# Own-engine waits only at data dependencies, new rests by layer, an early product with p_2, and layer 2 opened in quarters

## The chip, the core and the metric

The kernel runs on one core of a Trainium2 chip. The metric is the time of one execution on the device, in microseconds (us). TensorE is called PE, VectorE DVE, ScalarE ACT, GpSimd POOL and SyncE SP. "Clock" is TensorE's granted clock: 1.0 is 2.4 GHz, 0.5 is 1.2 GHz.

## What is computed

Two stacked networks over 256 tokens of width 2048, batch 1, all in float32. The first block has two layers; each is a modulation by a condition vector, an input projection of 6144 columns, a state-space mixer (S5) beside a differential attention, and an output projection. The second block has one layer: an RWKV-7 mixer beside a latent attention (MLA), an output projection, a convolutional feed-forward, and a product with a per-layer embedding `p_2`. Cut to the lines that matter here:

```python
for l in range(DEPTH):                                   # DEPTH = 2
    mod = c_act @ w_ada[l] + b_ada[l]
    shift, scale, gate = jnp.split(mod, 3, axis=-1)
    h = rms_norm(x, norm_g[l]) * (1.0 + scale[:, None, :]) + shift[:, None, :]
    proj = h @ w_in[l]
    u, z_s, q, k, v, z_a = jnp.split(proj, splits, axis=-1)
    y_s = s5_mixer(u, ...) * jax.nn.silu(z_s)
    y_a = diff_attention(q, k, v, ...) * jax.nn.silu(z_a)
    x = x + gate[:, None, :] * (jnp.concatenate([y_s, y_a], axis=-1) @ w_out[l])
x = rms_norm(x, final_g)
# second block
u = rms_norm_2(h, pre_mix_norm[i])
z = u @ w_in[i]
y_rw, y_mla = rwkv7_mixer(z_rw, ...), mla_mixer(z_mla, ...)
mix = (g_rw * (y_rw @ w_branch_rw[i]) + g_mla * (y_mla @ w_branch_mla[i])) @ w_out[i]
h = h + rms_norm_2(mix, post_mix_norm[i])
u = rms_norm_2(h, pre_ffn_norm[i])
up = causal_dwconv(u @ w_up[i], conv_w[i], conv_b[i])
gate, val = jnp.split(up, 2, axis=-1)
f = (gelu(gate) * val) @ w_down[i]
h = h + rms_norm_2(f, post_ffn_norm[i])
e = p[i] @ w_ple[i]
h = h + rms_norm_2(sigmoid(h @ w_ple_gate[i]) * e, ple_norm[i])
```

## The kernel before

**Products.** Activations lie transposed: 16 row blocks of 128 features by 256 tokens. Every large matrix is streamed as halves of 128x1024 numbers, eight 128x128 blocks each. ACT writes the high part of a half (`hi`, line 944) and DVE the rest (`lo`, line 941), and PE makes three products per block, high by high, high by rest, rest by high (`mm`, lines 988 and following). "A block" below is these three products of 128x256. Four halves can be split ahead of the one in use (`NS = 4`); the high part is made three halves ahead, the rest one beat later (`split_ahead`, `rest`).

**The order is written out beforehand.** `Timeline.run` makes one list of beats, and each engine's program walks through that list and emits its own part of each beat. All five queues are in order, so a beat's place in the list decides what stands in front of what on each engine. `stream(...)` lays a projection block by block. After every `per` blocks it calls `bg()` once, and each background generator (S5, its tail, attention, the next layer's modulation, RWKV, MLA) advances by one round. A generator adds a beat and then yields as many rounds as its "rest" says: with `per=2` one round of rest puts two blocks of product between two steps of a chain. `drain(...)` runs rounds with no product between them until the generator has ended.

**Rests.** They are tuples in `s5_prepare` (9 steps), `s5_follow` (8), `attention` (15) and `rwkv` (15 steps, for each of 8 pairs of heads), the same for both layers. PE's part of attention stands at steps 0, 7, 9 and 13, that of `s5_follow` at 0, 2, 4 and 6, that of `rwkv` at 0, 3 to 14. `s5_phases` places a DVE step and, some rounds later, three sines on ACT. After `rwkv` come `rw_seq` and `rw_post` (group norm: means, squares, variances, a root, scaling), and `drain(gr)` stands behind the stream they lie in.

**Order of the blocks.** An ordinary projection takes all 16 row blocks k of one tile of 128 columns, then the next tile. `PAIRS` names streams whose first two tiles are taken in halves: tile 0 with k 0 to 7, tile 1 with k 0 to 7, then k 8 to 15 of both. `QUADS` names streams whose first four tiles are taken in quarters: k 0 to 3 of four tiles, then k 4 to 7, and so on. Layer 2's input projection (`("w_in", 48)`) is in `PAIRS`.

**Waits on the own engine.** On ACT and DVE, every instruction but the splits calls `Port.begin()` (line 924), which waits until the newest earlier instruction of that engine has told of its end. `wait_ge` adds the waits on others. The splits (`apart_high`, `apart_low`) have none on their own engine.

**Between w_out2 and w_up.** After `w_out2` come the norm's sums (`rms`), `recip`, then for four groups of rows `scale`, `post` (the sum into x), four `hf` (the split of the new rows) and `sqf` (squares). The product with `p_2` (`w_ple`, 32 blocks) lies between `w_up`'s second half and `w_down1`; its operand is split at `w_up`'s end.

Of the kernel before, what the change touches and what calls it, by code (L numbers as in the profile page):

```python
# [173 lines left out]
MO = BK  # L174
_c = Cursor(BASE)
FO, FT, EM, PP = (_c.alloc(n) for n in (4096, 1536, 4096, 512))
FH = NF

# [63 lines left out]


# [42 lines left out]
PAIRS = (("w_in", 48), ("w_in2", 0), ("w_up", 0))  # L286

QUADS = (("w_pg", 0),)
# [11 lines left out]
class Timeline:  # L300
# [160 lines left out]
    def stream(self, name, l, u0, n0, nt, nk, per=8, late=None):  # L461
# [3 lines left out]
        for blk in range(nt * nk):  # L465
# [9 lines left out]
            if blk % 8 == 0:  # L475
                if (name, n, k) == ("w_up", 87, 8):
                    self.spared = p
                    for i in range(2):
                        self.add("part", "p", i)
# [16 lines left out]
            if k == nk - 1:  # L496
                held.append(t)
            if late is not None and blk == (71 if quads else 39):
# [42 lines left out]
    def s5(self, l):  # L541
# [8 lines left out]
        for x in self.s5_prepare(l, 0):  # L550
            yield
        for x in self.s5_phases(l, 0):
# [3 lines left out]
        for _ in range(6):  # L556
# [36 lines left out]
    def s5_phases(self, l, p):  # L593
        for _ in range(10 if p else 0):
            yield
        self.add("s5_phase", l, p)
        for _ in range(4):
# [14 lines left out]
    def s5_prepare(self, l, b):  # L612
        for i, rest in enumerate((1, 2, 2, 5, 3, 4, 1, 2, 0)):
# [4 lines left out]
    def s5_follow(self, l, b):  # L618
        for i, rest in enumerate((2, 3, 1, 5, 2, 3, 1, 2)):
# [35 lines left out]
    def rwkv(self):  # L655
# [74 lines left out]
    def run(self):  # L730
# [35 lines left out]
        for l in range(2):  # L766
# [15 lines left out]
            self.mod_rest = 2  # L782
# [3 lines left out]
            self.mod_rest = 5  # L786
# [10 lines left out]
            self.mod_rest = 2  # L797
# [93 lines left out]
class Op:  # L891


    def __init__(self, port, ins, chained=True):
        self.port, self.ins, self.told, self.chained = port, ins, False, chained

    def then_inc(self, sem, *keys):
# [3 lines left out]
        if self.chained:  # L901
            p.newest, self.told = (sem, p.n[sem]), True
# [4 lines left out]
class Port:  # L907


    def __init__(self, signals, name, e, m, in_order):  # L910
# [1911 lines left out]
```

## Time and profile before

| | |
|---|---|
| median of 3 runs | 3105.74 us (3104.97 to 3106.44) |
| the profiled execution | 3101.39 us |
| its span, first to last instruction | 3099.6 us |
| PE busy | 2911.4 us, 94% of the span |
| DVE busy | 2148.8 us, 69% |
| ACT busy | 1535.5 us, 50% |
| mean granted clock | 0.976 |

PE is the busiest engine by far, but "busy" contains stretches at half clock. The parts of the page and the views on which the prediction rests stand below, in its order.

### The profile page before, as it was taken

The numbers are of one execution on the slowest core, as the hardware profiler recorded it, in microseconds if no ns is written. First come the engines' busy times: TensorE is split into PE (matmuls) and PEld (weight loads), VectorE is DVE, ScalarE is ACT, GpSimd is POOL, SyncE is SP. The second block draws the span as 40 slices with busy tenths as digits, with TensorE's granted clock in tenths as the row PEclk, the third lists the DMA queues.
The fourth block names the chain that finished last, engine by engine and source line by source line (L and its number), as shares of the span: only waits on it lengthen the run. The fifth ranks groups of instructions, "written<-read, shape, count | busy, mean of one in ns | idle before, by whom it ended". The sixth has DMA issues, their size and how long they took to land.

```text
span 3099.6 us, 59134 instructions
## 1 busy us (share of the span) xinstructions
PE 2911.4 (94%) x24112; PEld 2695.1 (87%) x24112; DVE 2148.8 (69%) x3498; ACT 1535.5 (50%) x2404; POOL 284.4 (9%) x488
## 2 busy tenths in 40 slices
PE   6899999998999999999999999999899999999987
PEld 2578777788988889999888888999899999999987
DVE  6367777687788877766665667675888746887465
ACT  3335555365555655644343434545555544555454
POOL 0012212100122220200000010010000000000000
PEclk9899999998999999999999999999999999999999
DMA  9887776884645455554333334555455555555543
GB/s 376 309 264 256 248 266 232 286 287 158 179 153 164 155 182 194 177 181 157 107 108 110 115 117 137 163 178 184 134 190 185 186 184 180 181 187 177 184 151 116
DMA packets 168223, 580.91 MB, mean 187 GB/s; under 512 B 40272, under 2 KB 40304, under 8 KB 155536
## 3 DMA queue, kind: packets, MB, share of 16 engines
q1 hardware_dynamic: 146784, 525.40, 51.1%
q0 software_dynamic: 20592, 48.26, 5.1%
q8 instruction: 190, 3.11, 0.4%
q10 hardware_dynamic: 576, 3.47, 0.3%
q14 instruction: 81, 0.66, 0.1%
HBM read 555.22 MB, written 21.76 MB: 186 GB/s over the span
## 4 chain that ended last, share of the span: by engine, by line
PE 68%; DVE 15%; DMA 7%; ACT 5%; issue 4%; SPq 1%; POOL 0%; DVEq 0%; ACTq 0%
PE acc L988 67%; DVE arena L948 6%; ACT arena L985 3%; DVE upper L948 2%; DVE arena L958 1%; DMA arena<-in_w_ada 1%; DMA arena<-scr_k 1%; DVE rounded L941 1%; DMA arena<-in_w_in 1%; DMA scr_k<-arena 1%; DVE upper L958 1%; PE acc L991 1%; DMA upper<-in_w_ada 1%; ACT L985 1%; ACT upper L985 1%
## 5 line engine op out<-in xcount | busy, mean ns | idle before, releaser
L988 PE MATMUL acc<-rounded 128*128 128x256 f32 x14688 | 1913.1, 289 | 33.4 <-issue 14.3
L988 PEld LDWEIGHTS acc<-rounded 128*128 128x128 f32 x14688 | 1820.8, 194 | 117.1 <-issue 88.0
L944 ACT ACTIVATE rounded<-arena 128x1024 fp32r<-128x1024 f32 x802 | 847.7, 1059 | 735.4 <-PE acc L988 554.5
L941 DVE TENSOR_TENSOR rounded<-arena,rounded 128x1024 fp32r<-128x1024 f32 x802 | 974.8, 1225 | 247.0 <-ACT rounded L944 246.7
L988 PEld LDWEIGHTS acc<-upper_rounded,rounded 128*128 128x128 f32 x4560 | 551.8, 193 | 16.2 <-issue 14.0
L988 PE MATMUL acc<-upper_rounded,rounded 128*128 128x256 f32 x4560 | 557.7, 284 | 1.4 <-DVE rounded L941 0.9
L985 ACT ACTIVATE arena<-arena 128x256 f32<-128x256 f32 (+4 forms) x477 | 251.3, 527 | 226.3 <-DVE arena L948 143.1
L948 DVE TENSOR_TENSOR arena<-arena 128x256 f32<-128x256 f32 (+5 forms) x458 | 244.0, 533 | 46.2 <-ACT arena L985 33.2
L948 DVE TENSOR_TENSOR arena<-acc,arena 128x256 f32<-128x256 f32 (+4 forms) x270 | 117.2, 434 | 222.7 <-PE acc L988 213.2
L988 PE MATMUL acc<-arena 128*32 128x512 f32 (+8 forms) x1550 | 214.5, 487 | 51.4 <-DVE arena L948 23.0
L958 DVE SCALAR_TENSOR_TENSOR arena<-arena 128x256 f32<-128x256 f32 (+6 forms) x465 | 208.1, 448 | 51.0 <-ACT arena L985 35.3
L985 ACT ACTIVATE arena<-acc 128x256 f32<-128x256 f32 (+3 forms) x275 | 103.0, 374 | 199.1 <-PE acc L988 186.7
L988 PE MATMUL acc<-upper 128*128 128x128 f32 (+7 forms) x1568 | 184.9, 300 | 12.9 <-DVE upper L948 8.3
L988 PEld LDWEIGHTS acc<-arena 128*32 128x32 f32 (+3 forms) x1550 | 85.5, 140 | 114.5 <-DMA arena<-in_w_ada 46.2
L988 PEld LDWEIGHTS acc<-upper 128*128 128x128 f32 (+4 forms) x1568 | 144.5, 168 | 33.4 <-DVE upper L948 10.1
L985 ACT ACTIVATE upper<-acc 128x256 f32<-128x256 f32 (+4 forms) x176 | 88.0, 500 | 142.8 <-PE acc L988 100.8
L985 ACT ACTIVATE arena<-acc,arena 128x256 f32<-128x256 f32 (+1 forms) x148 | 63.3, 428 | 81.0 <-PE acc L988 76.0
L988 PE MATMUL acc<-upper,arena 64*64 64x64 f32 (+4 forms) x482 | 62.4, 352 | 28.2 <-DMA upper<-in_w_ada 8.2
L938 POOL DMA_DIRECT2D arena<-scr_k x128 | 77.3, 620 | 106.7 <-DMA scr_k<-arena 106.2
L991 PE MATMUL acc<-arena 128*128 128x128 f32 x384 | 71.0, 279 | 16.7 <-ACT arena L985 13.1
L948 DVE TENSOR_TENSOR upper<-upper,acc 128x512 f32<-128x512 f32 (+2 forms) x48 | 33.1, 689 | 76.8 <-PE acc L988 76.0
L938 POOL DMA_DIRECT2D scr_g<-arena x56 | 30.4, 545 | 517.8 <-DVE arena L962 270.1
(94 smaller groups left out, 1260.2 us busy)
## 6 DMA issues: line engine op xcount, KB each, us to landing
arena<-in_w_in SPq DMA_DIRECT2D x328, 512.0 KB, 4.6
arena<-in_w_ada SPq DMA_DIRECT2D x88, 1024.0 KB, 5.4
arena<-in_w_up SPq DMA_DIRECT2D x176, 512.0 KB, 4.1
arena<-in_w_down SPq DMA_DIRECT2D x88, 512.0 KB, 3.9
arena<-in_w_outa SPq DMA_DIRECT2D x32, 512.0 KB, 6.7
arena<-in_w_glu SPq DMA_DIRECT2D x32, 512.0 KB, 6.2
arena<-in_w_outm SPq DMA_DIRECT2D x32, 512.0 KB, 4.6
arena<-in_w_out SPq DMA_DIRECT2D x32, 512.0 KB, 4.3
```

The source lines that it names most:

```text
L938: self.e.dma_start(out, in_).then_inc(self.signals.sems[sem], 16)
L941: return Op(self, self.e and self.e.tensor_tensor(o, a, b, SUB), False)
L944: return Op(self, self.e and self.e.activation(o, a, ACT.Copy), False)
L948: return self.put(self.e and self.e.tensor_tensor(o, a, b, op))
L958: return self.put(self.e and self.e.scalar_tensor_tensor(out=o, in0=a, scalar=s, in1=b, op0=o1, op1=o2))
L985: return self.put(self.e and self.e.activation(o, a, f, scale=scale, **kw))
L988: return self.put(self.e and self.e.matmul(o, l, r, start=start, stop=stop, skip_group_check=True))
L991: return self.put(self.e and self.e.transpose(o, i, self.m.con("ident")))
```

## The change

- `Port.begin()` goes. DVE and ACT wait for their own engine only where a `settle()` is written out (64 places on DVE, and one at the end of ACT's program) or where a keyed wait names the instruction whose data is used (for example `("parts", l, b)`, `("aa", i)`, `("scaled", tag, g)`).
- The rests become tables, by layer for S5 and attention. `s5_phases` of layer 2 starts only when tile 0 of layer 2's input projection is evacuated. The modulation's rest (`mod_rest`) is 2 throughout; it was 2, 5, 2.
- Layer 2's input projection goes from `PAIRS` to `QUADS`, and its weights are packed accordingly.
- `w_ple` moves up between `w_out2` and `w_up`. Its beats surround those of the norm and of the first three groups of rows; the last group and all four squares come after eight blocks of `w_up`. The load and the split of `p_2` move ahead of that. Buffers move: `MO` to `AR`, the squares to `SQF`, `p_2`'s parts to `PT`.

```diff
-PAIRS = (("w_in", 48), ("w_in2", 0), ("w_up", 0))
-
-QUADS = (("w_pg", 0),)
+PAIRS = (("w_in2", 0), ("w_up", 0))
+
+QUADS = (("w_in", 48), ("w_pg", 0))
+
+S5_PREP = ((0, 1, 3, 6, 1, 6, 1, 2, 0),
+    (1, 2, 2, 4, 3, 3, 3, 1, 0))
+S5_RUN = ((1, 3, 1, 6, 2, 3, 2, 1),
+    (1, 4, 3, 6, 2, 1, 1, 1))
+S5_PHASE = ((13, 5),
+    (17, 2))
+S5_START = (6, 8)
+ATTENTION = ((1, 2, 4, 2, 3, 2, 4, 1, 3, 1, 1, 2, 2, 2, 1),
+    (1, 1, 2, 1, 2, 2, 4, 1, 5, 2, 2, 3, 3, 2, 1))
+RWKV = (1, 3, 3, 6, 3, 4, 2, 2, 2, 1, 2, 2, 2, 4, 1)
+MOD_REST = (2, 2, 2)
...
+        while l and ("w_in", 1, 0) not in self.marks:
+            yield
         for x in self.s5_phases(l, 0):
...
-        for i, rest in enumerate((1, 2, 2, 5, 3, 4, 1, 2, 0)):
+        for i, rest in enumerate(S5_PREP[l]):
...
-        for i, rest in enumerate((2, 3, 1, 5, 2, 3, 1, 2)):
+        for i, rest in enumerate(S5_RUN[l]):
...
-            for i, rest in enumerate((2, 2, 2, 2, 2, 2, 4, 2, 2, 2, 1, 2, 2, 2, 1)):
+            for i, rest in enumerate(ATTENTION[l]):
...
-            for s, rest in enumerate((1, 2, 3, 5, 3, 3, 2, 2, 2, 2, 2, 2, 2, 2, 1)):
+            for s, rest in enumerate(RWKV):
...
-        self.stream("w_out2", 0, 0, 0, 16, 16)
-        self.rms("mo", ("w_out2", 0, 15))
-        self.ready("w_up", 0)
-        self.add("recip", "mo")
-        for g in range(4):
-            self.scaled("mo", g)
+        self.add("ff_first")
+
+        def parts():
+            for i in range(2):
+                self.add("part", "p", i)
+
+        self.stream("w_out2", 0, 0, 0, 16, 16, between={63: parts})
+
+        def root():
+            self.add("recip", "mo")
+            self.scaled("mo", 0)
+
+        def rows(g):
             for k in range(4 * g, 4 * g + 4):
                 self.add("hf", k)
-            self.add("sqf", g)
-        self.add("ff_first")
+            if g < 3:
+                self.scaled("mo", g + 1)
+
+        self.stream("w_ple", 0, 0, 0, 16, 2, between={
+            4: lambda: self.rms("mo", ("w_out2", 0, 15)), 8: root, 13: lambda: rows(0), 21: lambda: rows(1),
+            29: lambda: rows(2)})
+        self.ready("w_up", 0)
...
-        self.stream("w_up", 0, 0, 0, 44, 16, late=late)
+        self.stream("w_up", 0, 0, 0, 44, 16, late=late, between={8: last_rows})
         self.stream("w_down0", 0, 0, 0, 16, 22)
         self.stream("w_up", 0, 44, 44, 44, 16)
-        self.stream("w_ple", 0, 0, 0, 16, 2)
...
-    def begin(self):
-        if self.in_order and self.op is not None:
-            if not self.op.told:
-                self.op.then_inc(self.name + "_step")
-            if self.e is not None:
-                self.wait_value(*self.newest)
+    def settle(self):
+        if self.newest.told is None:
+            self.newest.then_inc(self.name + "_step")
+        if self.e is not None:
+            self.wait_value(*self.newest.told)
...
     def tt(self, o, a, b, op):
-        self.begin()
         return self.put(self.e and self.e.tensor_tensor(o, a, b, op))
```

## Rows read from the trace of the kernel before

**Rows 1.** The page's part 1: busy us of PE, its share, instructions.
```profile
PE 2911.4 (94%) x24112; PEld 2695.1 (87%) x24112; DVE 2148.8 (69%) x3498; ACT 1535.5 (50%) x2404; POOL 284.4 (9%) x488
```
**Rows 2.** Windows: length, busy us (x instructions) per engine, clock, DMA share, GB/s.
```profile
113.00:730.00 617.00, 583.07 (x4886) 491.85 (x4886) 442.99 (x771) 303.60 (x534) 100.74 (x171) 0.98 0.78 260
730.00:758.00 28.00, 18.32 (x85) 15.22 (x85) 21.78 (x46) 17.87 (x30) 0.00 (x0) 0.70 0.17 57
758.00:1140.00 382.00, 355.56 (x3100) 324.65 (x3099) 309.36 (x532) 214.59 (x410) 83.75 (x144) 0.98 0.55 167
1447.00:1893.00 446.00, 422.40 (x3634) 387.46 (x3633) 287.67 (x447) 176.04 (x268) 35.74 (x65) 0.98 0.34 111
1893.00:1922.00 29.00, 29.00 (x268) 27.68 (x267) 18.02 (x28) 12.56 (x15) 5.09 (x8) 1.00 0.49 159
2183.00:2207.00 24.00, 14.07 (x81) 12.88 (x80) 19.78 (x28) 14.98 (x25) 0.30 (x1) 0.76 0.08 27
2207.00:2835.00 628.00, 628.00 (x5221) 627.71 (x5221) 470.52 (x742) 318.03 (x412) 0.24 (x1) 1.00 0.57 184
```
**Rows 3.** PE's waits, 113 to 730 us: total us, times, longest.
```profile
PE acc L988 <- DMA arena<-scr_k: 9.9, 6, 2.6
...
PE acc L988 <- DMA arena<-in_w_ada: 6.5, 4, 2.2
...
PE acc L988 <- DMA upper<-scr_u: 1.7, 1, 1.7
```
**Rows 4.** PE's waits, 758 to 1140 us: the one on a DMA.
```profile
PE acc L988 <- DMA arena<-scr_k: 0.9, 1, 0.9
```
**Rows 5.** PE's waits, 1447 to 1893 us: the two longest.
```profile
PE acc L988 <- DVE upper L948: 12.0, 12, 2.5
PE acc L988 <- DVE upper L958: 6.3, 5, 2.0
```
**Rows 6.** DVE's timeline, 2306 to 2308 us: start, us, instruction; L958 follows a split.
```profile
2305.46 1.22 DVE L941 TENSOR_TENSOR rounded<-arena,rounded 128x1024 fp32r<-128x1024 f32 x1
2306.59 0.42 DVE L958 SCALAR_TENSOR_TENSOR arena<-arena 128x256 f32<-128x256 f32 x1
```
**Rows 7.** DVE's timeline, 2185 to 2192 us: `scale` and `post` of the first group.
```profile
2186.24 1.22 DVE L948 TENSOR_TENSOR arena<-arena,acc 128x1024 f32<-128x1024 f32 x1 [0.86 <-PE acc L988]
2187.50 1.22 DVE L948 TENSOR_TENSOR arena<-arena 128x1024 f32<-128x1024 f32 x1
```
**Rows 8.** ACT's timeline, 2299 to 2302 us: a split and two others.
```profile
2299.42 1.07 ACT L944 ACTIVATE rounded<-arena 128x1024 fp32r<-128x1024 f32 x1 [1.81 <-PE acc L988]
2300.39 0.40 ACT L985 ACTIVATE upper_rounded<-arena 128x256 fp32r<-128x256 f32 x1
2300.89 0.60 ACT L985 ACTIVATE arena<-arena 128x256 f32<-128x256 f32 x1
```
**Rows 9.** ACT's timeline, 730 to 736 us.
```profile
731.15 1.28 ACT L985 ACT_TABLE_LOAD   x1
732.45 3.02 ACT L985 ACTIVATE arena<-arena 128x256 f32<-128x256 f32 x5
```
**Rows 10.** PE's timeline from 728 us; the last product before ended at 729.99.
```profile
735.98 1.02 PE L988 MATMUL acc<-arena 128*128 128x1 f32 x4 [5.99 <-DVE arena L948]
...
740.50 4.96 PE L988 MATMUL acc<-rounded 128*128 128x256 f32 x13 [1.73 <-issue]
```
**Rows 11.** PE's timeline, 744 to 758 us: where block 24 of layer 2 starts.
```profile
757.65 0.62 PE L988 MATMUL acc<-rounded 128*128 128x256 f32 x3 [0.28 <-DVE rounded L941]
```
**Rows 12.** DVE's timeline, 749.8 to 751.2 us: one k of beat `h`.
```profile
749.86 0.48 DVE L958 SCALAR_TENSOR_TENSOR rounded<-upper,arena,rounded 128x256 fp32r<-128x256 f32 x1
750.38 0.48 DVE L958 SCALAR_TENSOR_TENSOR upper<-arena,acc 128x256 f32<-128x256 f32 x1
750.97 0.48 DVE L958 SCALAR_TENSOR_TENSOR rounded<-upper,arena,rounded 128x256 fp32r<-128x256 f32 x1
```
**Rows 13.** PE's timeline, 2183 to 2207 us: first and last start on w_up.
```profile
2190.75 2.90 PE L988 MATMUL acc<-rounded 128*128 128x256 f32 x12 [4.60 <-issue]
...
2204.69 2.61 PE L988 MATMUL acc<-rounded 128*128 128x256 f32 x11 [1.69 <-DVE rounded L958]
```
**Rows 14.** The timeline, 2832 to 2852 us: PE inside w_ple.
```profile
2841.85 8.17 PE L988 MATMUL acc<-rounded 128*128 128x256 f32 x66 [2.89 <-ACT arena L985]
```
**Rows 15.** PE's waits, 1960 to 2183 us: MLA's transposes behind DVE.
```profile
PE acc L991 <- DVE upper L953: 5.5, 8, 0.7
```

More of the change, by code:

```diff
@@ L173 @@
 GT = TMPS
-MO = BK
+MO = AR
 _c = Cursor(BASE)
@@ L459, in ready, with stream @@
         self.split_ahead(self.halves + NS - 1)
-    def stream(self, name, l, u0, n0, nt, nk, per=8, late=None):
+    def stream(self, name, l, u0, n0, nt, nk, per=8, late=None, between=None):
         held = []
@@ L475, in stream @@
             if blk % 8 == 0:
[L476 to L479, printed above, removed]
                 p = self.halves
@@ L497, in stream @@
                 held.append(t)
+            if between is not None and blk in between:
+                between[blk]()
             if late is not None and blk == (71 if quads else 39):
@@ L555, in s5 @@
             yield
-        for _ in range(6):
+        for _ in range(S5_START[l]):
             yield
@@ L593, in s5_phases @@
     def s5_phases(self, l, p):
-        for _ in range(10 if p else 0):
+        for _ in range(S5_PHASE[l][0] if p else 0):
             yield
         self.add("s5_phase", l, p)
-        for _ in range(4):
+        for _ in range(S5_PHASE[l][1]):
             yield
@@ L833, in run, with last_rows @@
             self.add("part", "mx", n)
-        self.stream("w_out2", 0, 0, 0, 16, 16)
-        self.rms("mo", ("w_out2", 0, 15))
-        self.ready("w_up", 0)
-        self.add("recip", "mo")
-        for g in range(4):
-            self.scaled("mo", g)
+        self.add("ff_first")
[7 more added lines that the diff above has]
+        def rows(g):
             for k in range(4 * g, 4 * g + 4):
                 self.add("hf", k)
-            self.add("sqf", g)
-        self.add("ff_first")
+            if g < 3:
[4 more added lines that the diff above has]
+        self.ready("w_up", 0)
+        def last_rows():
+            rows(3)
+            for g in range(4):
+                self.add("sqf", g)
         self.bgs.append(self.square_sums())
@@ L1553, in xs @@
         act.wait_ge("x_dve", ("fo", g))
-        act.wait_ge("mm", ("out", tl.out_of["w_ple", 0, 15].o))
+        act.wait_ge("mm", ("out", tl.out_of["w_up", 0, 87].o))
         act.act(m.HT4(g)[0], V(X + 1024 * g, 1024), ACT.Copy).then_inc("part_act", ("xs", g))
@@ L1572, in part @@
                 "cq": ("w_in2", 0, 67)}
-        if tag == "p":
-            act.wait_ge("mm", ("half", tl.spared))
-        elif isinstance(tag, str) and (tag != "cq" or j >= 4):
+        if isinstance(tag, str) and tag != "p" and (tag != "cq" or j >= 4):
             act.wait_ge("mm", ("out", tl.out_of[free[tag]].o))
-        if tag == "cq":
+        if tag == "ya":
+            act.wait_ge("mla_act", ("y", j))
+        elif tag == "cq":
             act.wait_ge("mla_dve", ("cq", j))
@@ L1940, in recip @@
         if tag in ("x0", "hf"):
-            dve.recip(V(RS, 256), V(RS, 256))
+            dve.recip(V(RS, 256), V(RS, 256)).then_inc("norm_dve", ("root", tag))
         else:
@@ L1984, in h @@
                 dve.wait_ge("norm_pe", ("over", ("x", 0)))
+            else:
+                dve.wait_ge("norm_dve", ("root", "x0"))
+            dve.wait_ge("mod_dve", ("gp", l, j // 4))
             root = B(3, 0, 256) if l else V(RS, 256)
@@ L2313, in mla @@
         if i == 2:
+            dve.wait_ge("mla_dve", ("s", h))
             for qb in range(2):
                 dve.red(V(MNM + qb, 1), V(MPR + 128 * qb, 128 * (qb + 1)), MAX)
+            dve.settle()
+            for qb in range(2):
                 x = dve.ts(V(MNM + 2 + qb, 1), V(MNM + qb, 1), -192 ** -0.5, None, MUL)
@@ L2341, in add_square @@
         dve.wait_ge("sq_act", ("ev", t.o))
+        if not first:
+            dve.wait_ge("sum_dve", summed[to])
         x = dve.copy(V(to, 256), s) if first else dve.tt(V(to, 256), V(to, 256), s, ADD)
         x.then_inc("sum_dve", ("ev", t.o))
+        summed[to] = "ev", t.o
     def ev(t, ph):
@@ L2352, in ev @@
             dve.wait_ge("mm", ("out", t.o))
+            dve.wait_ge("norm_dve", ("root", "hf") if t.name == "w_up" else "roots")
             dve.tt(V(at, 256, np_=np_), B(b, 0, 256, np_=np_), V(RS if t.name == "w_up" else RSH, 256, np_=np_),
```

154 lines of the change are left out of this document (111 added, 43 removed).

## The prediction

> **What bounds the kernel now.** I read the page's part 1 first: PE is busy 2911.4 us of 3099.6 [rows 1], so 188 us of it are idle and no other engine comes near. Then the windows by stage [rows 2]. From 2207 to 2835 us PE has no idle time and the clock is 1.00: 5221 products in 628 us, 0.120 us each, 0.36 us per block. Such a stretch (both projections up, down, and layer 2's output) can't get shorter by anything in this change. What can are four kinds of place. (a) Bodies with chains beside the product: 113 to 730 us with 617 - 583.1 = 33.9 us of idle, 758 to 1140 with 26.4, 1447 to 1893 (RWKV) with 23.6, each at clock 0.98, so about 2% of the stretch lost once more. (b) Openings, where all of PE waits for a norm: 730 to 758 with clock 0.70, 2183 to 2207 with clock 0.76. (c) MLA, where PE waits 8 times, 5.5 us in all [rows 15]. (d) The start (to 113 us), bound by loads, and the end. Last I read in the timeline what ends each wait. PE's queue is in order, so a chain step placed too early stops the whole product.
>
> **What an own-engine wait costs.** The splits have no such wait, the others do. On DVE the L958 behind a split starts at 2306.59, 0.09 us before the split ends at 2306.68 [rows 6]: the split's end had already been covered by an older signal. `post` behind `scale` starts at 2187.50, 0.04 us after 2187.46 [rows 7]. So a wait that goes saves about 0.13 us of a back-to-back chain. On ACT the pair without it overlaps by 0.10 us, that with it stands 0.10 apart [rows 8]: 0.2 us. Where the engine idles anyway the saving is nothing.
>
> The Trainium skill speaks against this ("VectorE: DVE Perf Modes", The DRAIN you can't avoid): leaving out the semaphore between two vector instructions wins nothing, since the pipe drains anyway. The rows do not agree, 0.04 us behind against 0.09 us ahead; by the rule the sum would be that of the rival "own waits are free" below.
>
> **Opening of layer 2 (730 to 758).** PE's first sum waits 5.99 us [rows 10]. In front of the square on ACT stand three sines of S5's phase step and their table load [rows 9]: three of five instructions, 3/5 x 3.02 = 1.8 us, and 1.28 us. The new condition on tile 0 moves them behind the opening: 3.1 us. Then beat `h` runs 16 times at 750.97 - 749.86 = 1.11 us [rows 12], two DVE instructions of 0.48 us with gaps of 0.04 and 0.11. Both waits go; at an overlap of 0.09 the step is 0.78 us, 0.33 less, 5.3 us for 16. I take 4, since ACT sits between the two. Block 24 starts at 757.65 [rows 11], behind the split of the fourth half, which stands behind all 16 `h` on DVE. That stays so in quarters: they let PE do its 24 blocks (72 x 0.12 = 8.7 us) before the last rows come, but give little alone. Gain 3.1 + 4 = 7 us; bounds 3 (sines only, less ACT) and 11 (27.7 us now less 8.7, with the clock back earlier).
>
> **w_ple moved (2183 to 2207, 2835 to 2850).** Now 24 us pass in which PE makes 81 - 8 = 73 products worth 8.8 us; the loss is 15.2 us, and 1 more while the clock comes back. The first rows are there at 2190.75, the last only at 2204.69 and after [rows 13]. In w_ple itself PE waits 2.89 us [rows 14]. Sum of losses 19. After the change PE has 32 blocks of w_ple and 23 of w_up before it needs the last row: 55 x 0.36 = 19.8 us. DVE's first `scale` starts 3.2 us into the window now [rows 7] and 1 us later then, behind blocks 0 to 8. A group of rows takes (2204.69 - 2190.75)/3 = 4.65 us now [rows 13] and, with two waits less, about 4.4; between the groups stand five weight splits of 2306.59 - 2305.46 = 1.13 us [rows 6], since w_ple needs weights too. The last row comes after 4.2 + 4 x 4.4 + 5 x 1.13 = 27.4 us, and the loss is 27.4 - 19.8 = 7.6, say 8. What is late next is DVE's last group. ACT gets 16 evacuations in the same window; they have five banks of slack. Gain 19 - 8 = 11 us; bounds 5 (DVE six us later, behind ACT's evacuations) and 16 (two splits less in the way, first rows earlier).
>
> **MLA.** The chain scores, maximum, exponential, reciprocal, scaling loses four own waits of 0.13 on DVE and one of 0.2 on ACT, 0.7 us, and PE waits 5.5/8 = 0.69 us per head [rows 15]. Most goes: 4.5 us; bounds 2 and 5.5.
>
> **Body of layer 2 (758 to 1140).** 26.4 us idle, of which 0.9 behind a DMA [rows 2, 4]; 25.5 behind ACT and DVE, and 0.02 x 382 = 7.6 us by the clock. Chains get shorter (about five own waits of DVE and five of ACT per attention head, 1.6 us), and rests move: from `pt` on ACT to the output product 5 rounds for 2, from `yn` to its transposes 3 for 2, before S5's state product 6 for 5. But from scores to transposes there are 13 rounds for 16, and between ACT's copy of y and PE's transposes of it 1 for 3. I take half: 13 + 3 = 16 us; bounds 2 and 30.
>
> **Bodies of layer 1 and its output (113 to 730).** 33.9 us, 18.1 of it behind DMAs [rows 3]. From the write of the taps to the product that reads them there are 2 + 11 rounds before and after, so scr_k's 9.9 us mostly stay (2 saved by earlier ACT); the modulation's unit comes 3 rounds sooner behind its load, so 6.5 us can rise by 2. Of the other 15.8 us half: 8, and clock 2. Gain 10; bounds 0 and 20.
>
> **RWKV (1447 to 1922).** The rests add up to 38 for 34: 4 rounds x 2 blocks x 0.36 = 2.9 us more cover per pair. Step 13 has 4 for 2, so the 12.0 us behind DVE (about 1 us for each of 8, and the sequence) mostly go; 6.3 us behind L958 [rows 5] shrink by a third with shorter chains. Some 15 of 23.6 us go. Against it: step 9 has 1 for 2, 0.3 us each, 2.4; and 8 x 4 = 32 rounds more push 54 blocks' worth of the tail past the stream. Of `rw_post`, now under 29 us with PE fully busy [rows 2], all runs in `drain(gr)` without cover. PE's own work there goes on; its waits for ACT's root with a table load (1.28 us in [rows 9]) and DVE's recip and scaling show, about 6.5 us. Net 6; bounds -8 and +15. A wait taken from one place is partly given back here.
>
> **Rest.** Last opening and end: eight `scale` and `post` pairs and splits lose one wait each where they don't depend, 2 us; start 1 us. 3 us, bounds 1 and 5.
>
> **Sum.** 7 + 11 + 4.5 + 16 + 10 + 6 + 3 = 57.5 us. The profiled execution took 3101.4 us (span 3099.6, 1.8 around it) and becomes 3043.9. The runs' median is 4.3 us higher, 3105.7, and becomes 3048.
>
> **Rivals.**
> - *Own waits are free* (DVE hides them). Then the opening gives 3, MLA 0, the rest 0, the w_ple move 10, the two bodies half: 3 + 10 + 13 + 6 = 32 us, 3074. Against it: the 0.13 us of [rows 6, 7]. 12%.
> - *Rests only move the waits.* The bodies and RWKV give nothing, since each step waits for a chain of fixed length: 7 + 11 + 4.5 + 3 = 25.5, 3080. For it: cover is taken from one step and given to another at equal sums in S5. 10%.
> - *The waits nearly all go.* 26 in layer 2, 22 in layer 1, 20 in RWKV, 23 at the openings, 7.5 else: 98 us, 3007. For it: a chain step needs only a microsecond or two of cover more. 14%.
> - *Shortened rests stop PE* (slower). In layer 2 three rounds less in 8 heads (17.3 us), two less in 16 S5 batches (23), RWKV's step 9 in 8 pairs (5.8), and `rw_post` bare, 64 blocks of cover (23): 69 us at full price, against 25.5 of gains that don't hang on rests. It decides from 37% of that price; at half it is 3106 + 34.5 - 25.5 = 3115. Against it: chains lose 1 to 2 us themselves. 5%.
> - *Nothing to be measured*: DVE's longer queue at w_up and the bare `rw_post` eat what the rest gives. 4%, about 3104.
>
> **How the numbers follow.** The forecast has 55%. All bounds at one end would give 5 or 102 us, 3101 or 3004; not all fall on one side, and its own range is 3015 to 3085. The range 3008 to 3084 takes in the first two rivals and half of the third, and leaves out 16%. A measurement here can tell about 0.2%, 6 us, from no change. Faster 91%, same 4%, slower 5%.
>
> **What would show it.** DVE pairs such as `post` behind an independent instruction should stand at -0.09 us. The sum before layer 2 should wait 3 us, not 6, and `h` repeat at 0.8 us. No wait inside w_ple, and PE's products should fill 2183 to 2195 at clock 1.0; the window before w_up's last group should lose 8 us. MLA's wait should be under 0.2 us per head. RWKV's steps should stay without 1 us waits, with a new idle of some 6 us at `rw_post`. I am wrong if `h` still takes 1.1 us, if attention's transposes in layer 2 wait more than now, or if idle time in 1893 to 1922 grows beyond 15 us.

## The result and the profile after

| | before | after |
|---|---|---|
| median, us | 3105.35 | 3007.85 (3007.30 to 3008.11) |
| profiled execution, us | 3101.4 | 3007.8 |
| its span, us | 3099.6 | 3006.0 |

The kernel before was run again beside it, hence its median. The ratio is 0.9686, with a 95% interval of 0.9672 to 0.9701: 97.5 us less, where 57.5 were forecast. The time is just below the range; it is that of the rival "the waits nearly all go" (3007).

The page's part 1, after:

```profile
PE 2891.0 (96%) x24112; PEld 2684.4 (89%) x24112; DVE 2076.3 (69%) x3498; ACT 1485.9 (49%) x2406; POOL 291.1 (10%) x488
```

Against [rows 1] PE makes the same 24112 products. Its idle time fell from 188.2 to 115.0 us, 73.2 less, and its busy time by 20.4. The sum is 93.6, the difference of the spans; every microsecond of idle time that went took 0.28 us of busy time with it. Only a small part of the 20.4 is the clock: its mean over the span is 0.976 before and 0.977 after, so some 74 us of full clock are lost before (0.024 x 3099.6) and 69 after. The last section says what is known of the rest.

The windows by stage, after. Columns as in [rows 2].

```profile
113.00:710.50 597.50, 577.52 (x4872) 486.92 (x4870) 421.66 (x761) 293.44 (x536) 102.80 (x171) 0.98 0.81 268
710.50:728.99 18.49, 12.88 (x83) 12.11 (x82) 16.79 (x43) 11.77 (x22) 0.00 (x0) 0.82 0.17 55
728.99:1080.20 351.21, 346.01 (x3091) 319.15 (x3092) 297.40 (x539) 205.93 (x415) 88.47 (x144) 0.99 0.59 180
1386.00:1821.50 435.50, 427.76 (x3664) 393.79 (x3664) 271.51 (x435) 173.86 (x271) 36.04 (x65) 1.00 0.37 120
1821.50:1869.70 48.20, 43.05 (x374) 40.69 (x375) 32.64 (x59) 19.72 (x39) 5.37 (x8) 0.79 0.33 105
2106.30:2123.00 16.70, 15.98 (x130) 15.39 (x128) 15.26 (x21) 13.52 (x32) 0.00 (x0) 1.00 0.30 97
2377.80:2758.00 380.20, 380.20 (x3171) 380.20 (x3170) 260.50 (x396) 185.35 (x237) 0.00 (x0) 1.00 0.57 184
```

The third line is the body of layer 2: 5.2 us idle in 351.2 us, where the same stretch of before (757.65 to 1137.10) has 25.5 in 379.4. The fifth, RWKV's tail, is the one stretch of these that became worse: clock 0.79, where [rows 2] have 1.00 for 1893 to 1922. The last, with no idle time, did not change, as forecast.

Because everything shifts, I compare stretches bounded by the same products: each ends with the last product of the projection named. The table also has the two experiments that divide the change, "waits alone" (`waits_only`) and "rests and order alone" (`rests_only`). Each column adds up to its span.

| stretch, us | before | waits alone | rests and order alone | after |
|---|---|---|---|---|
| layer 1, input projection | 555.5 | 549.2 | 550.8 | 543.2 |
| layer 1, output | 174.5 | 171.9 | 169.7 | 167.3 |
| opening of layer 2, to block 24 | 27.7 | 22.0 | 22.8 | 18.5 |
| body of layer 2 | 379.4 | 351.9 | 364.0 | 351.2 |
| layer 2, output | 140.3 | 139.3 | 139.0 | 138.8 |
| w_in2, first part | 169.9 | 167.1 | 169.9 | 167.0 |
| w_in2, second part, and q_up (RWKV) | 492.5 | 480.5 | 488.1 | 483.7 |
| kv_up and MLA | 98.3 | 93.2 | 98.4 | 93.1 |
| rest of MLA, w_out2 | 145.1 | 143.4 | 145.3 | 143.5 |
| norm, half of w_up, w_ple | 286.7 | 283.7 | 275.2 | 271.5 |
| down, half of w_up | 380.1 | 380.1 | 380.1 | 380.2 |
| second down, w_pg, end | 249.6 | 248.1 | 251.1 | 248.0 |
| span | 3099.6 | 3030.3 | 3054.5 | 3006.0 |

PE's waits in the body of layer 2, before and then after (engine and line, what was waited for, us in all, times, longest):

```profile
PE acc L991 <- ACT arena L985: 9.4, 7, 3.6
PE acc L988 <- DVE upper L948: 4.7, 3, 1.9
PE acc L988 <- ACT arena L985: 4.3, 3, 3.6
PE acc L991 <- ACT rounded L944: 3.0, 2, 2.0
PE acc L988 <- DVE upper L958: 2.1, 2, 1.1
PE acc L988 <- ACT upper L985: 1.6, 1, 1.6
...
```
```profile
PE acc L1007 <- ACT arena L1001: 5.0, 2, 3.9
PE acc L1004 <- DVE rounded L972: 1.7, 1, 1.7
PE acc L1007 <- DVE arena L980: 0.2, 1, 0.2
```

Before, twenty waits of up to 3.6 us lay over eight heads and 16 batches: not one per head. Behind eleven of them DVE or ACT had worked for 5 to 19 us without a break; behind the others the engine had itself just waited. After, three are left in the body, and the 1.7 us belong to the opening. The two behind ACT (3.89 and 1.15 us) came with the new order: ACT had waited 2.37 and 3.27 us for POOL, where in the body of before it waits for POOL once, 0.8 us. POOL's short step of attention's norm stood there behind four loads for S5, and these behind the write that they read. ACT's part before it was done by 919.9, and POOL came to it at 926.5:

```profile
924.04 2.40 POOL L969 DMA_DIRECT2D arena<-scr_k  x4 [2.96 <-DMA scr_k<-arena]
926.97 1.56 POOL L972 TENSOR_TENSOR arena<-arena 128x2 f32<-128x2 f32 x1
928.56 0.63 ACT L1001 ACTIVATE arena<-acc,arena 128x128 f32<-128x128 f32 x2 [2.37 <-POOL arena L972]
```

The chains themselves, after: DVE's timeline in the opening of layer 2 (answers [rows 12]) and at the first group of `scale` and `post` before `w_ple` (answers [rows 7]).

```profile
716.42 0.48 DVE L980 SCALAR_TENSOR_TENSOR rounded<-upper,arena,rounded 128x256 fp32r<-128x256 f32 x1
716.81 0.47 DVE L980 SCALAR_TENSOR_TENSOR upper<-arena,acc 128x256 f32<-128x256 f32 x1
717.20 0.48 DVE L980 SCALAR_TENSOR_TENSOR rounded<-upper,arena,rounded 128x256 fp32r<-128x256 f32 x1
...
2111.73 1.23 DVE L972 TENSOR_TENSOR arena<-arena 128x1024 f32<-128x1024 f32 x1
2112.88 1.22 DVE L972 TENSOR_TENSOR arena<-arena,acc 128x1024 f32<-128x1024 f32 x1
```

The `h` step is 717.20 - 716.42 = 0.78 us, as forecast, for 1.11. `scale` behind `post` starts 0.08 us before `post` ends (2111.73 + 1.23 = 2112.96), where it stood 0.11 behind. `post` itself reads what `scale` before it wrote; its wait stays, and it starts 0.03 us after that one's end.

### The profile page after: what moved, and what is told of

Read it like the earlier page. It is cut to its first block, busy times and chain, and to the rows that moved or that the text cites. A ratio compares the mean times of both kernels' runs of the same rounds, so it can differ in the third digit from the quotient of the medians.

```text
span 3006.0 us, 57317 instructions
## 1 busy us (share of the span) xinstructions
PE 2891.0 (96%) x24112; PEld 2684.4 (89%) x24112; DVE 2076.3 (69%) x3498; ACT 1485.9 (49%) x2406; POOL 291.1 (10%) x488
## 4 chain that ended last, share of the span: by engine, by line
PE 86%; DMA 5%; DVE 5%; ACT 1%; issue 1%; SPq 1%; POOL 1%; DVEq 0%; ACTq 0%
PE acc L1004 84%; DMA arena<-in_w_ada 2%; DVE arena L972 2%; PE acc L1007 2%; DVE rounded L972 1%; DMA scr_k<-arena 1%; SPq L969 1%; DMA upper<-in_w_ada 1%; DVE upper L972 1%; DVE upper L980 1%; DMA scr_u<-upper 0%; DMA arena<-scr_k 0%; DVE rounded L980 0%; ACT arena L1001 0%; POOL arena L969 0%
## 5 line engine op out<-in xcount | busy, mean ns | idle before, releaser
L1004 PE MATMUL acc<-rounded 128*128 128x256 f32 x14592 | 1883.6, 287 | 20.6 <-issue 9.0
L1004 PEld LDWEIGHTS acc<-rounded 128*128 128x128 f32 x14592 | 1795.7, 193 | 100.4 <-issue 83.0
L1001 ACT ACTIVATE rounded<-arena 128x1024 fp32r<-128x1024 f32 (+1 forms) x862 | 875.3, 1022 | 749.5 <-PE acc L1004 677.1
L972 DVE TENSOR_TENSOR rounded<-arena,rounded 128x1024 fp32r<-128x1024 f32 (+1 forms) x830 | 985.0, 1199 | 260.0 <-ACT rounded L1001 259.5
L1004 PE MATMUL acc<-upper_rounded,rounded 128*128 128x256 f32 x4656 | 570.2, 284 | 2.7 <-DVE rounded L972 2.0
L1001 ACT ACTIVATE arena<-arena 128x256 f32<-128x256 f32 (+3 forms) x473 | 233.0, 515 | 170.7 <-DVE arena L972 116.1
L972 DVE TENSOR_TENSOR arena<-acc,arena 128x256 f32<-128x256 f32 (+5 forms) x270 | 113.9, 432 | 238.1 <-PE acc L1004 237.3
L972 DVE TENSOR_TENSOR arena<-arena 128x256 f32<-128x256 f32 (+4 forms) x455 | 234.6, 526 | 36.9 <-ACT arena L1001 28.9
L1004 PE MATMUL acc<-arena 128*32 128x512 f32 (+7 forms) x1542 | 214.4, 486 | 39.3 <-DMA arena<-in_w_ada 24.8
L980 DVE SCALAR_TENSOR_TENSOR arena<-arena 128x256 f32<-128x256 f32 (+5 forms) x465 | 205.3, 446 | 29.9 <-ACT arena L1001 21.8
L1004 PEld LDWEIGHTS acc<-upper 128*128 128x128 f32 (+4 forms) x1568 | 143.7, 170 | 23.7 <-issue 9.1
```

The costliest lines, as they stand in the source:

```text
L972: return self.put(self.e and self.e.tensor_tensor(o, a, b, op))
L980: return self.put(self.e and self.e.scalar_tensor_tensor(out=o, in0=a, scalar=s, in1=b, op0=o1, op1=o2))
L1001: return self.put(self.e and self.e.activation(o, a, f, scale=scale, **kw))
L1004: return self.put(self.e and self.e.matmul(o, l, r, start=start, stop=stop, skip_group_check=True))
```

## The experiments

Theories at the start: **W**, the own-engine waits carry most of the gain; **R**, the rests and the new order do. The kernels below differ in waits, rests and order alone. Each set ran on one chip, beside the kernel before, which had medians of 3104.0 to 3105.4 us in all four sets, with single runs from 3097 to 3117. The changed kernel was not run again in them: differences from its 3007.85 us go from set to set, and some 6 us are within the intervals of the ratios.

**Set 1: dividing the change.**

`waits_only`: the kernel before, its beats and rests untouched, with the new rule for own-engine waits. One of its changes against the kernel before:

```diff
     def tt(self, o, a, b, op):
-        self.begin()
         return self.put(self.e and self.e.tensor_tensor(o, a, b, op))
```

> The kernel before with the new waits alone: own-engine waits of DVE and ACT only at data dependencies, but the old rests (RWKV, S5, attention, modulation), pairs in layer 2, the old start of its phases and w_ple at its old place; the list of beats is that of the kernel before. Theory W (shorter chains did it: they now fit under the old rests): the bodies of both layers and RWKV give back some 35 us, MLA 5, the layer 2 opening 5, the one before w_up 1, together 3058 us. Theory R (the new rests did it, waits matter only at openings and in MLA): about 3093 us.

Measured: 3031.3 us, ratio 0.9761 (0.9739 to 0.9783). This is well below both expectations, 3058 and 3093. Theory W holds and was too small: 74 us of the 97.5 come with the waits alone.

`rests_only`: the changed kernel with the old waits back on both engines (the splits again have none). The method that every other instruction calls first:

```diff
+    def begin(self):
+        if self.name in ('act', 'dve') and self.op is not None:
+            if self.op.told is None:
+                self.op.then_inc(self.name + "_step")
+            if self.e is not None:
+                self.wait_value(*self.op.told)
```

> The changed kernel, but every DVE and ACT instruction except the weight splits again waits for the newest earlier one of its engine, as before. Order, rests, quarters and w_ple as changed. Theory W: the order alone brings 13 us by w_ple, 4 by the sines, 15 by rests: 3072 us. Theory R: 3030 us. If both parts are independent, this run's gain and that of waits_only add up to 97 us; if each hides the same stall, they add up to more.

Measured: 3056.5 us, ratio 0.9845 (0.9818 to 0.9871), a gain of 49, between the two expectations. The two parts add up to 123 where together they give 97.5: about 25 us of stalls can be removed by either. The table shows where. In the body of layer 2 the rests give 379.4 - 364.0 = 15.4 us while the waits are there and 351.9 - 351.2 = 0.7 once they are gone. In RWKV it is 492.5 - 488.1 = 4.4 us with the waits. Without, the columns show a loss of 483.7 - 480.5 = 3.2, but that is within the variation: seven profiles with these rests and without the waits take 478.8 to 483.7 us for this stretch, three with the old rests (`waits_only`, `old_rests`, `rwkv_old`) 480.5 to 481.5. The move of `w_ple` doesn't overlap: 11.5 with, 12.2 without.

`old_rests`: the changed kernel with all the rests of before.

```diff
-RWKV = (1, 3, 3, 6, 3, 4, 2, 2, 2, 1, 2, 2, 2, 4, 1)
-MOD_REST = (2, 2, 2)
+RWKV = (1, 2, 3, 5, 3, 3, 2, 2, 2, 2, 2, 2, 2, 2, 1)
+MOD_REST = (2, 5, 2)
...
```

> The changed kernel with the old tables of rests for S5, attention, RWKV and the modulation; new waits, quarters, w_ple early and the later start of layer 2's phases stay. Theory W: 10 to 20 us slower than the changed kernel, 3023 us. Theory R: 45 us slower, 3053 us.

Measured: 3014.1 us (3013.8 to 3014.4), 6 us over the changed kernel and below both expectations. By these two runs all the new rests together are worth about 6 us, and the later sets put even that in doubt.

`rwkv_old`: only RWKV's old rests.

> The changed kernel with RWKV's old rests (sum 34 for 38). My sum: the 1 us waits at step 14 come back in part (8 us) and the bare tail of 6.5 us goes, with its half clock some 10 us: 6 us slower by the forecast, 3014 us. Rival, the longer rests cost as much at the tail as they bring: equal or faster, 3000 to 3008 us, with the wait of step 14 under 0.3 us because its chain is shorter now.

Measured: 3005.5 us (3004.5 to 3006.4), in the span of the rival: 2.4 us less than the changed kernel. The rival's second sign did not come: the wait before step 14 is 0.64 us in eight places, not under 0.3. The windows of the two stretches of this kernel (second part of w_in2, q_up):

```profile
1384.80:1848.20 463.40, 446.35 (x3893) 411.20 (x3893) 290.94 (x473) 180.69 (x282) 40.71 (x72) 0.99 0.36 116
1848.20:1866.30 18.10, 17.67 (x147) 17.41 (x146) 13.01 (x21) 12.84 (x28) 0.56 (x1) 1.00 0.63 201
```

With the longer rests the first stretch takes 446.9 us and the second 36.8: 483.7 against 481.5. What the longer rests save before the stream ends comes back in the tail. The 2 us more are within the variation given above. PE's timeline of the tail in the changed kernel:

```profile
1829.43 1.92 PE L1004 MATMUL acc<-upper 64*64 64x32 f32 x32 [2.17 <-DVE arena L972]
1831.28 1.65 PE L1004 MATMUL acc<-rounded 128*128 128x256 f32 x6
1832.72 5.53 PE L1004 MATMUL acc<-arena 128*128 128x256 f32 x16
...
1856.34 10.04 PE L1004 MATMUL acc<-upper_rounded,rounded 128*128 128x256 f32 x70 [1.99 <-DVE rounded L972]
```

The tail's granted clock (1821.5 to 1869.7) is 0.79. In the groups of products by shape, `rw_post`'s 64 products take 278 ns each in the kernel before (1900 to 1966 us) and 349 in the changed one (1821 to 1895 us), of both the line of that shape:

```profile
L988 PE MATMUL acc<-arena,upper 128*64 128x128 f32 x64 | 4.4, 278 | 0.0
```
```profile
L1004 PE MATMUL acc<-arena,upper 128*64 128x128 f32 x64 | 5.6, 349 | 0.9 <-DVE upper L986 0.8 <-DVE arena L972 0.2
```

**Set 2: which engine, and the order.**

`dve_bound` and `act_bound`: as `rests_only`, with `('dve',)` or `('act',)` in `begin`.

> The changed kernel with the old waits back on DVE alone: before each DVE instruction other than a weight split, DVE waits for its own newest one; ACT stays as changed. With the waits back on both engines the time was 3056.5 us, with none 3007.9, so the waits of both cost 48.7 us together under these rests. Theory D (DVE's waits carry most: chains of S5, attention and RWKV have more DVE than ACT steps, MLA's 0.6 us a head and the h steps of 1.1 us are DVE's): 33 to 42 us, 3041 to 3050. Rival A (ACT's waits are 0.2 us against 0.13 and carry as much): 20 to 27 us, 3028 to 3035. MLA's waits should be back at about 5 us for D and for A alike.

> The changed kernel with the old waits back on ACT alone. Theory D (DVE's waits carry most): 7 to 15 us more than the changed kernel, 3015 to 3023. Rival A (as much as DVE's): 20 to 27 us, 3028 to 3035. If the two engines' waits hide the same stalls of PE (the later of two chains decides), the gains of this kernel and of the one with DVE's waits back add up to less than 48.7 us; if they lie in one chain after another, to 48.7.

Measured: 3042.9 us (+35.0 against the changed kernel) and 3018.2 (+10.4). Theory D holds. The two make 45.4 of 48.7, so the waits of the two engines hide little of each other's. MLA was expected to be the same for both, and is not: PE's waits there are 4.3 us with DVE's,

```profile
PE acc L1031 <- DVE upper L993: 4.3, 8, 0.5
```

and with ACT's, as in the changed kernel, the view of MLA's stretch lists none. There the expectation was wrong: that chain is DVE's.

`ple_old`: `w_ple` at its old place.

```diff
-        self.stream("w_out2", 0, 0, 0, 16, 16, between={63: parts})
+        self.stream("w_out2", 0, 0, 0, 16, 16)
...
         self.stream("w_up", 0, 44, 44, 44, 16)
+        self.stream("w_ple", 0, 0, 0, 16, 2)
```

> The changed kernel with w_ple back at its old place behind the second half of w_up, and the norm of w_up's rows opened as before. All waits and rests stay as changed. The forecast gave the move 11 us with bounds of 5 and 16. From the spans of before with only the waits changed (267.8 from the last product of w_out2 to the middle of w_up's and 15.9 for w_ple) against the changed kernel (271.5 for both) the move is worth 12 us: 3018 to 3022. Rival (the shorter chains of DVE carry most of it, as w_ple is then short of losses): 5 us, 3013.

Measured: 3017.0 us (3014.0 to 3018.5), +9.2. By the windows, the two stretches that hold this work take 267.3 + 15.8 = 283.1 us for 271.5, 11.6 more:

```profile
2103.60:2370.90 267.30, 260.46 (x2130) 259.40 (x2131) 224.76 (x377) 145.13 (x199) 0.54 (x1) 0.98 0.54 174
2751.00:2766.80 15.80, 13.13 (x99) 12.93 (x98) 10.40 (x16) 9.87 (x22) 0.00 (x0) 0.89 0.51 165
```

The move is worth 9 to 12 us.

`pairs`: layer 2 opened in halves.

```diff
-PAIRS = (("w_in2", 0), ("w_up", 0))
-QUADS = (("w_in", 48), ("w_pg", 0))
+PAIRS = (("w_in", 48), ("w_in2", 0), ("w_up", 0))
+QUADS = (("w_pg", 0),)
...
```

The weights are packed for halves again.

> The changed kernel with the first 48 units of layer 2's input projection opened in halves as before, not in quarters. The forecast said that quarters give little alone. Theory L (block 24 stands behind the last row's split in either order): under 1.5 us, 3007 to 3009.5. Rival Q (in quarters PE works through four blocks' first quarter while the rows come, so halves start the last part later): 3 to 5 us, 3011 to 3013. The opening from the last product of layer 1 to block 24 is 18.5 us with quarters.

Measured: 3004.6 us (3000.8 to 3008.9), no slower. Its whole input projection of layer 2 takes 369.1 us for 369.7, and PE's timeline shows the same 74 products and block 24 after 18.0 us for 18.5:

```profile
711.15 12.51 PE L1004 MATMUL acc<-rounded 128*128 128x256 f32 x74 [1.68 <-issue]
723.93 21.28 PE L1004 MATMUL acc<-rounded 128*128 128x256 f32 x174 [0.27 <-DVE rounded L972]
```

The quarters gave nothing: theory L.

**Set 3: what an own-engine wait delays.** Is it the chain that PE waits for (C), or whatever stands before it in the engine's queue (Q)? The waits are put back, on DVE and ACT and in both layers, only in attention's or only in S5's steps. Of `own_att`, on DVE:

```diff
     for beat, *of in tl.beats:
         if beat in play:
+            dve.bound = beat in ('att',)
             play[beat](*of)
```

> The changed kernel with the old own-engine waits back, on DVE and ACT, only in attention's steps (8 heads in each layer); everything else stays as changed. All own waits back cost 48.7 us, about 27 of them in the stretch of the two layers (to 1083 us), where PE's waits behind attention's steps in layer 2 grew from 5.2 to 12.9 us and those behind S5's from 0 to 1.7. Theory C (a wait of PE grows by what the chain that it waits for loses itself): 10 to 16 us, 3018 to 3024. Rival Q (what counts is any instruction that stands before the chain in the engine's queue, of whichever chain): 5 to 9 us, 3013 to 3017.

> The changed kernel with the old own-engine waits back, on DVE and ACT, only in S5's steps (16 batches in each layer). Theory C (a wait of PE grows by what the chain that it waits for loses itself): PE hardly waits for S5's steps, so 1 to 5 us, 3009 to 3013, with attention's waits as in the changed kernel. Rival Q (any instruction before the chain in the queue counts; S5 has more instructions than attention): 9 to 16 us, 3017 to 3024, and the waits behind attention's transposes grow although attention's own steps are unchanged.

Measured: `own_att` 3015.4 us (3009.0 to 3018.3), +7.5; `own_s5` 3014.0 us (3011.7 to 3016.8), +6.2. Neither theory alone: the first lies in Q's span, the second between the two. As ratios to the kernel before they are 0.9708 (0.9686 to 0.9729) and 0.9706 (0.9686 to 0.9727), intervals that overlap with the changed kernel's 0.9672 to 0.9701; the whole times alone would not carry the reading. In the body of layer 2 they cost 357.6 - 351.2 = 6.4 and 355.4 - 351.2 = 4.2 us, of 12.8 for all waits. Layer 2's whole input projection takes 376.3 and 373.6 us, against 366.2 to 370.7 in the five profiles, the changed kernel's among them, in which layer 2 is as changed and without own waits. PE's waits there with S5's own waits back:

```profile
PE acc L1032 <- ACT arena L1026: 7.0, 3, 5.0
PE acc L1029 <- DVE rounded L977: 1.9, 1, 1.9
PE acc L1032 <- DVE arena L999: 1.6, 2, 1.1
PE acc L1029 <- DVE upper L989: 0.8, 2, 0.6
```

The first and third lines are attention's transposes. Attention's own steps are those of the changed kernel, where these lines read 5.0 and 0.2. The waits of the third line stand behind 13.5 and 14.6 us of unbroken DVE work. Most of the first line is again the wait of ACT for POOL (2.69 and 3.68 us, where the changed kernel has 2.37 and 3.27). So a wait in one chain delays the other, through the shared queues: Q's mechanism exists, beside C's, and its size is a few microseconds here.

**Sets 3 and 4: the rests one by one.** Single lines of the tables are put back.

`l1_old` (layer 1's old rests), `l2_old` (layer 2's), `mod5` (`MOD_REST = (2, 5, 2)`):

> The changed kernel with the old rests of S5 and attention in layer 1 alone (its modulation rest and everything in layer 2 and RWKV stay as changed). With all old rests the end of layer 1 came at 718.3 us against 710.5, and the whole run took 6 us more; with RWKV's old rests alone 2.4 us less. Theory L (layer 1's rests are the only ones of use): 6 to 9 us more, 3014 to 3017. Rival (the start's loads vary by that much and the rests do nothing): within 2 us, 3006 to 3010.

> The changed kernel with the old rests of S5 and attention in layer 2 alone. The forecast gave a part of 16 us to them together with the shorter chains. With all old rests the projection of layer 2 took 370.8 us for 369.7, with only the waits changed 373.8. Theory N (with the waits gone the rests of layer 2 do nothing): within 2 us of the changed kernel, 3006 to 3010. Rival (they carry the 6 us of all old rests): 3012 to 3015.

> The changed kernel with the old rest of 5 rounds (for 2) between the units of the modulation during layer 1's output. With all old rests layer 1 ended 7.8 us later (718.3 for 710.5), with S5's and attention's old rests in layer 1 alone 1.6 us later (712.1). Theory M (the modulation's rest carries this: the 16 units must be through before layer 2 opens): 4 to 7 us more, 3012 to 3015. Rival (the two stretches differ by the loads of the start alone): within 2 us, 3006 to 3010.

Measured: 3001.3 (2998.1 to 3004.7), 3009.0 (3006.1 to 3012.6) and 3006.7 us (2999.5 to 3012.9): `l1_old` lies below both expectations, the other two in their rivals' span or theory N's. None of them makes the kernel measurably slower; the 6 us of `old_rests` found no owner. For layer 2 its whole projection takes 369.2 us with the old rests for 369.7, and its output 140.0 for 138.8. For layer 1 there is no such figure: its input projection ended between 535.6 and 549.2 us in the profiles of the kernels with all the waits gone, more than any of these edits is worth, and PE's waits for the modulation's loads alone vary over this projection between 26 and 31 us.

`nomark`: without the condition on tile 0.

```diff
-        while l and ("w_in", 1, 0) not in self.marks:
-            yield
```

> The changed kernel without the condition that holds layer 2's phase step of S5 back until tile 0 of its projection has begun. The forecast gave the condition 3.1 us: three sines of 0.60 us and a table load of 1.28 us in front of the square. Theory S (they stand there again): 3 us more, PE's first wait before layer 2 grows from 1.6 to about 4.7 us as it is in the kernel with only the waits changed, 3010 to 3012. Rival (the step comes later by itself, since the rest before it is 17 for 10 rounds): no difference, 3006 to 3010.

Measured: 3004.6 us (3002.4 to 3009.2), no loss. PE's first sum before layer 2 waits 2.49 us for 1.58, not 4.7:

```profile
714.15 0.61 PE L1002 MATMUL acc<-arena 128*128 128x1 f32 x4 [2.49 <-DVE arena L970]
```

The rest of 17 rounds for 10 had moved most of the sines already; in `l2_old`, with the condition and a rest of 10, the wait is 1.57. Either of the two nearly suffices.

`pairs_rw34` and `best`: attempts to beat the changed kernel; `best` has layer 1's old rests as well.

> A version meant to beat the changed one: layer 2 opened in halves as before, and RWKV's rests (1, 2, 3, 6, 2, 3, 2, 2, 2, 1, 2, 1, 2, 4, 1), whose sum is 34 as before, with the 4 rounds before step 14 kept. With the old rests of sum 34 the tail of RWKV behind the stream was 18 us instead of 37 for q_up, but eight steps waited 0.64 us each before step 14. If both parts keep their worth: 5.1 us of those waits go, 1 to 2 us come at step 3 with shorter cover, so 3 us below the kernel with RWKV's old rests: 3002, and 3001 with the halves. If the waits only move to another step: 3005.

> The changed kernel with layer 2 opened in halves, layer 1's old rests of S5 and attention, and RWKV's rests (1, 2, 3, 6, 2, 3, 2, 2, 2, 1, 2, 1, 2, 4, 1). Alone or in pairs these gave -6.5 (layer 1's rests) and -3.7 us (the other two). If the worths add up: 2997 to 2999. If layer 1's figure was the variation of the start's loads: 3002 to 3005. Over 3007 would mean that they do harm together.

Measured: 3004.2 us (3003.9 to 3008.1) and 3003.9 us (2996.5 to 3012.9). The ratios to the kernel before, 0.9679 (0.9659 to 0.9699) and 0.9673 (0.9646 to 0.9699), can't be told from the changed kernel's 0.9686. In `pairs_rw34` the wait before RWKV's step 14 went, and 1.6 us in eight waits came up before step 12, where I had cut a round: 482.8 us for w_in2's second part and q_up, against 483.7 in the changed kernel and 481.5 in `rwkv_old`. The attempt moved a wait.

## Why the prediction was wrong

The direction, the places and the prices per instruction held, if roughly. What failed is the term for the bodies of the two layers, by one decision, taken twice: "I take half" of the waits, against a count of own waits in attention's chain alone (1.6 us a head) that put S5's at nothing.

- **Price of an own wait.** The 0.78 us of the `h` step came as forecast. The 0.13 us came from `post` behind `scale`, whose wait is one that stays; those that went measure 0.14 us on average on DVE in the body of layer 2 and 0.15 over the whole kernel, so the price was near, by luck in part. By the rule of the Trainium skill ("VectorE: DVE Perf Modes", The DRAIN you can't avoid) leaving the semaphore out wins nothing. `waits_only` does not agree: 74 us. The same section says that a next operation that is not held starts earlier, and the 0.08 us of overlap agree with that.
- **Opening of layer 2**: 7 forecast, 27.7 - 18.5 = 9.2 measured. Sines: the wait fell from 5.99 to 1.58 us; of this 4.71 to 1.58 is the moved phase step (3.1, as forecast), the rest the waits. That the quarters give little was right.
- **w_ple**: 11 forecast, 15.2 measured, at the upper bound of 16. The move gives 11.6 to 12.2 of it and the waits the rest. The mis-sized part is the last group of rows: it was to come 27.4 us after the window's start and cost 8 us. A group with a split between takes 2123.98 - 2118.99 = 4.99 us, where I had 4.4 + 1.13 = 5.5, and it is ready at 2128.97 + 1.67 = 2130.6, 24.3 us after the start; PE waits only 1.2 and 0.7 us:

```profile
2118.99 1.67 DVE L980 SCALAR_TENSOR_TENSOR rounded<-arena,rounded 128x256 fp32r<-128x256 f32 x4
...
2123.98 1.67 DVE L980 SCALAR_TENSOR_TENSOR rounded<-arena,rounded 128x256 fp32r<-128x256 f32 x4
...
2128.97 1.67 DVE L980 SCALAR_TENSOR_TENSOR rounded<-arena,rounded 128x256 fp32r<-128x256 f32 x4
...
2124.12 3.13 PE L1004 MATMUL acc<-rounded 128*128 128x256 f32 x24 [1.16 <-DVE rounded L972]
2127.97 4.30 PE L1004 MATMUL acc<-rounded 128*128 128x256 f32 x30 [0.73 <-DVE rounded L972]
```

- **MLA**: 4.5 forecast, 4.7 measured (72.4 to 67.7); no wait of PE is listed there any more.
- **Body of layer 2**: 16 forecast, 28.2 measured; the largest error, 12 us. I shortened each head's chain by 1.6 us, 13 us for eight, and let half of the 25.5 us of waits go. 20.3 of them went, and 7.9 us of busy time, where I had 3 for the clock (by its records the clock is 3.9 of them). The own waits alone give 27.5.

  The step left out: an own wait doesn't only lengthen the chain that it is in, and S5's 16 batches have them too. What they took can be read from the records of this stretch in the kernel before and in `waits_only`, which have the same beats. I add up, between neighbours on an engine, the next start less the last end wherever that is under 0.15 us. On DVE the sum goes from +4.2 us to -17.8, since 157 more of the 432 instructions that are not splits now overlap with the one before; 188 still stand 0.03 us behind, as an instruction does whose wait stays. On ACT it goes from -7.1 to -29.9, with 134 more overlapping. That is 22 and 23 us of the two engines' time, 0.14 and 0.17 us each. How much of the 28.2 us came over the other chain's queue I can't divide: `own_att` and `own_s5` bring back 10.6 of 12.8 us, both partly over the other's chain.
- **Bodies of layer 1 and its output**: 10 forecast and 1 for the start, 19.5 measured. scr_k's waits were to stay at about 8 of 9.9 us, and fell to 2.5; the modulation's rose from 6.5 to 8.4, by the 2 forecast. After, from 110 to 710 us:

```profile
PE acc L1004 <- DMA arena<-in_w_ada: 8.4, 5, 2.8
PE acc L1007 <- ACT arena L1001: 5.8, 2, 4.9
PE acc L1004 <- DMA arena<-scr_k: 2.5, 2, 2.2
```

  Since this stretch varies by more than ten microseconds between kernels that differ little in it, a part of the 19.5 may be such variation; this stays open.
- **RWKV**: 6 net forecast, 492.5 - 483.7 = 8.8 measured. Its two halves were both there: stalls down, and a bare tail that costs (18.5 us more in q_up's stretch). What I had not seen is the split by cause. The waits alone give 12.0; with them gone the rests give nothing that stands out of the variation. `rw_post` waits less than feared (0.9 us for 6.5); the tail loses by the clock, 0.79, instead.
- **Rest**: 3 forecast with the start. Layer 2's output, w_in2's first part, kv_up, the rest of MLA, w_out2, the second down, w_pg and the end give 1.5 + 2.9 + 0.5 + 1.6 + 1.6 = 8.1 together: waits that I hadn't listed.

The errors are 12 in the body of layer 2, about 9 in layer 1, 4 at w_ple, 3 in RWKV, 2 at the opening and 6 in the rest, all of one sign: 36 us. Most hang on the same unknown, what shorter chains do to the waits (`waits_only` takes 69.3 us off the span, of 93.6), so they could not cancel, and adding half-way values for each as if they were independent made the range too narrow at its low end. Of the rivals, "rests only move the waits" was true of the rests once the waits were gone. "The waits nearly all go" meets the sum, in part by luck: of its 20 us in RWKV 8.8 came, of its 7.5 for all else 12.8, and 115 us of idle time are left.

## What to carry to other kernels

A cost paid at every instruction of a shared in-order queue is to be counted per instruction of the queue, not per step of the one chain that is looked at, and only for those that lose it: here 157 waits on DVE and 134 on ACT, 45 us of the two engines' time in a stretch of 379, where the chains of attention had suggested 13. Not all of a queue's instructions count: at 0.13 us for each of the 432 on DVE alone it would have been 56. Before hand-tuned delays are changed beside such a cost, take the cost out first: the new rests were worth 15 us in layer 2 with the waits and under 1 without, and 4 us in RWKV with them and nothing to be measured without. The engines that do little belong in the picture too: the longest waits left in layer 2 stand behind POOL. When several terms of a sum hang on the same unknown, the range has to move with it, all terms at once.

## What was unexpected of the hardware

- Waits cost more than their idle time. 73.2 us less of it brought 20.4 us of shorter busy time for the same products; with the waits alone it was 45.6 and 23.7 (PE busy 2887.7 in a span of 3030.3). The clock is the smaller part of the first figure: by its records PE was busy at 1.2 GHz for 109.5 us before, 100.0 after and 81.7 with the waits alone, and half of the differences is 4.8 and 13.9 us. A second part, as an estimate: the record of a product lasts 0.29 us where one starts every 0.12 us, so each break in the flow adds 0.17 us of busy time; the unbroken pieces of PE's work fell from 145 to 91 (9 us) and to 113 (5 us). The remainder, 4 to 7 us, is open.
- RWKV's tail without cover lost more by the clock than by waiting: 18.3 of the 43.1 us that PE is busy in it are at 1.2 GHz, worth 9 us, beside 48.2 - 43.1 = 5.2 us of idle time. This varies from profile to profile: over q_up's stretch the clock is 0.86 in the changed kernel and 0.94 in `pairs`, with the same rests.
- The own-engine waits cost the kernel more on DVE than on ACT (35 us against 10), though in the engines' own time they are not far apart: over the whole kernel the same sum over neighbours differs by 119 us on DVE between the changed kernel and `dve_bound`, and by 92 on ACT between it and `act_bound`. That ACT idles half of the time fits this; no run tests it as the reason.
